# One-core decoder layer: reordered updates, scans and bias products, and other buffers for two weight halves

## What is computed

```python
def reference(x, mem, ...):
    h = rms_norm(x, norm_pre_mix)
    y = mixing_block(h, ...)            # four groups of 256 columns, see below
    x = x + rms_norm(y, norm_post_mix)
    h = rms_norm(x, norm_pre_xa)
    y = cross_attention(h, rms_norm(mem, norm_mem), xa_wq, xa_wkv, xa_wo)   # 4 heads, 256 memory tokens
    x = x + rms_norm(y, norm_post_xa)
    h = rms_norm(x, norm_pre_ffn)
    gu = h @ ffn_w_in                   # 1024 -> 2 x 2816
    y = (silu(gu[..., :2816]) * gu[..., 2816:]) @ ffn_w_out
    return x + rms_norm(y, norm_post_ffn)

def mixing_block(h, ...):
    u_s5, p_ml, p_rw, p_mb = split_cols(h @ w_in, ...)
    y = [s5_mixer(u_s5), mlstm_mixer(p_ml), rwkv7_mixer(p_rw), moba_mixer(p_mb, rel_bias)]
    return rms_norm_per_group(concatenate(y)) @ w_out
```

## Time and profile before

| | |
|---|---|
| median of 3 executions | 520.66 us (520.61 to 520.70) |
| profiled execution | 520.58 us, span 518.8 us |
| PE busy | 487.5 us (94%) |
| DVE busy | 378.5 us (73%) |
| ACT busy | 261.8 us (50%) |
| POOL busy | 167.0 us (32%) |
| moved by DMA | 79.33 MB, 153 GB/s |

### The profile page before, as it was taken

How to read it: one execution, slowest core, us unless ns; L and a number is a source line. 1 busy time by engine, 2 the same in 40 slices (tenths; PEclk the granted TensorE clock), 3 DMA queues, 4 the chain that set the end, 5 groups by cost and what they waited for, 6 DMA issues and landing times.

```text
span 518.8 us, 8480 instructions
## 1 busy us (share of the span) xinstructions
PE 487.5 (94%) x3494; PEld 446.7 (86%) x3494; DVE 378.5 (73%) x445; ACT 261.8 (50%) x412; POOL 167.0 (32%) x101
## 2 busy tenths in 40 slices
PE   0799999979999999999999999999999999999985
PEld 0789889978899878878999988999999999988874
DVE  5676797997756889587756466699999999962114
ACT  3598864412622334666856557544445444443333
POOL 0040227297669360000000000244334433443540
PEclk9999999989999999999999999999999999999999
DMA  8937328022031222626373460275445555545502
GB/s 334 375 96 233 150 81 322 3 82 81 1 100 64 82 82 81 244 82 220 120 270 125 155 223 26 82 265 183 163 167 195 205 173 200 199 162 198 208 1 81
DMA packets 12358, 79.33 MB, mean 153 GB/s; under 512 B 1440, under 2 KB 2080, under 8 KB 3488
## 3 DMA queue, kind: packets, MB, share of 16 engines
q1 hardware_dynamic: 12320, 78.79, 42.5%
HBM read 76.95 MB, written 1.84 MB: 152 GB/s over the span
## 4 chain that ended last, share of the span: by engine, by line
PE 84%; DVE 8%; ACT 3%; issue 2%; DMA 1%; POOLq 0%; POOL 0%; SPq 0%; DVEq 0%; ACTq 0%
PE bank L381 82%; DMA ring<-weights 1%; DVE arena L1668 1%; ACT w_high L356 1%; DVE vx L1695 1%; DVE arena L1485 1%; POOLq L90 0%; POOL w_rest L362 0%; DVE arena L1660 0%; DVE we_rest L362 0%; DVE arena L1661 0%; DVE wk_rest L362 0%; DVE arena L1839 0%; DVE wm_rest L362 0%; PE bank L814 0%
## 5 line engine op out<-in xcount | busy, mean ns | idle before, releaser
L362 POOL TENSOR_TENSOR w_rest<-ring,w_high 128x1024 fp32r<-128x1024 f32 x21 | 50.8, 2418 | 202.6 <-ACT w_high L356 202.6
L356 ACT ACTIVATE w_high<-ring 128x1024 fp32r<-128x1024 f32 x66 | 69.4, 1058 | 72.7 <-PE bank L381 72.6
L381 PE MATMUL bank<-h_high,w_high 128*128 128x256 f32 x384 | 102.9, 283 | 0.0
L381 PE MATMUL bank<-h_rest,w_high 128*128 128x256 f32 x352 | 99.6, 283 | 0.0
L381 PE MATMUL bank<-h_high,w_rest 128*128 128x256 f32 x320 | 90.6, 283 | 0.0
L362 DVE TENSOR_TENSOR w_rest<-ring,w_high 128x1024 fp32r<-128x1024 f32 x39 | 49.8, 1282 | 37.4 <-ACT w_high L356 37.4
L381 PEld LDWEIGHTS bank<-h_high,w_high 128*128 128x128 f32 x384 | 71.7, 192 | 0.5 <-issue 0.4
L381 PEld LDWEIGHTS bank<-h_rest,w_high 128*128 128x128 f32 x352 | 67.6, 192 | 0.0
L381 PE MATMUL bank<-arena 128*128 128x128 f32 (+7 forms) x496 | 59.2, 300 | 6.5 <-DVE arena L1691 4.5
L381 PEld LDWEIGHTS bank<-arena 128*128 128x128 f32 (+3 forms) x496 | 52.8, 182 | 12.6 <-DVE arena L1691 5.1
L381 PEld LDWEIGHTS bank<-h_high,w_rest 128*128 128x128 f32 x320 | 61.4, 192 | 0.0
(11 more groups left out here) (323 smaller groups left out, 1230.6 us busy)
## 6 DMA issues: line engine op xcount, KB each, us to landing
ring<-weights SPq DMA_DIRECT2D x50, 1024.0 KB, 5.0
third_slot<-weights SPq DMA_DIRECT2D x15, 1024.0 KB, 5.1
cst<-consts SPq DMA_DIRECT2D x1, 1664.0 KB, 12.6
gain<-gains SPq DMA_DIRECT2D x3, 512.0 KB, 5.8
par<-params SPq DMA_DIRECT2D x1, 1168.0 KB, 14.9
kx<-x_t SPq DMA_DIRECT2D x1, 1024.0 KB, 4.9
vx<-mem_t SPq DMA_DIRECT2D x1, 1024.0 KB, 10.3
xres<-x_rows SPq DMA_DIRECT2D x1, 1024.0 KB, 10.4
```

The source lines that it names most:

```text
L356: nc.scalar.activation(split_half(i)[0], raw_half(i), ACT.Copy).then_inc(S["w_high"], 1)
L362: e.tensor_tensor(rest_, raw_half(i), high.bitcast(F32), ALU.subtract).then_inc(rest_done(i)[0], 1)
L381: return nc.tensor.matmul(out_, lhsT, rhs, start=start, stop=stop, skip_group_check=True)
```

## The change

- The constant `onehot` moves to the front of the second block and comes with a DMA of its own, 33 rows, between weight slots 0 and 1 (`onehot_in`). The bias products `rel0` to `rel3` run right behind `x_sumsq`, ahead of `rw_wag`. PE's waits for the other constants and parameters move to just before `rw_w`.
- POOL makes the level-3 mask before `rotate_back(0)`.
- DVE: one rest, `level_update(1)`, one rest and then `scan(0)`; mLSTM's masks ahead of `scan(1)`; `solution(1)` ahead of S5's sigmoid and product.
- The group sum of S5 stands behind tile 1 of `wout`, not behind tile 0.
- The last two halves of `ffn_w_out` get the buffers `w_kx` and `w_wo[0]` for their high and rest parts, and ACT's split of them waits for no earlier product.

```diff
 CONST, NCONST = columns([
-    ("ones", P), ..., ("half_pi", 1), ("ident", P), ...
+    ("ones", P), ..., ("half_pi", 1), ("onehot", 384), ("ident", P), ...
-    ("onehot", 384),
 ])
-CONST_FIRST = CONST["ident"][0]
+CONST_FIRST, CONST_MORE = CONST["onehot"]
...
             if H_WO + HALF_BUFS <= i < H_FIN:
                 return w_wo[i - H_WO - HALF_BUFS]
+            if i >= NHALF - 2:
+                return (w_kx, w_wo[0])[i - NHALF + 2]
             return w_mid[i % MID_BUFS] if i < H_LATE else w_late[(i - H_LATE) % HALF_BUFS]
...
-            if before >= start:
+            if before >= start and i < NHALF - 2:
                 user = half_user[before]
...
             mm(o[:, 0:T], const("ones"), sq_x[:, 0, :]).then_inc(full[0], 1)
-            split_channel_major(0, "rw_wag", 1, h_split, lambda j: pe.wait_ge(S["h_rest"], j + 1))
-            split_channel_major(1, "rw_k", 0, h_split)
-            pe.wait_ge(S["consts_in"], 16)
-            pe.wait_ge(S["params_in"], 16)
+            pe.wait_ge(S["onehot_in"], 16)
             for h in range(NH):
                 o = pe_open(pe, f"rel{h}", 4 + h)
                 mm(o[:, 0:384], prm("rel", 33)[:, h:h + 1].to_broadcast([33, P]), const("onehot", 33)).then_inc(full[4 + h], 1)
+            split_channel_major(0, "rw_wag", 1, h_split, lambda j: pe.wait_ge(S["h_rest"], j + 1))
+            split_channel_major(1, "rw_k", 0, h_split)
             split_channel_major(2, "rw_r", 1, h_split)
...
             o = v3(pe_open(pe, "rw_w", 2)[:, :], T)
+            pe.wait_ge(S["consts_in"], 16)
+            pe.wait_ge(S["params_in"], 16)
             pe.wait_ge(S["rw_low"], 1)
...
             def group_sums(kt):
-                if kt == 0:
+                if kt == 1:
                     group_sumsq("gn_s5", 0, 3)
...
             for n in range(NSLOTS):
+                if n == 1:
+                    sp.dma_start(cst[0:33, CONST_FIRST:CONST_MORE], consts_d[0:33, CONST_FIRST:CONST_MORE]).then_inc(S["onehot_in"], 16)
                 if n == 2:
-                    sp.dma_start(cst[:, CONST_FIRST:], consts_d[:, CONST_FIRST:]).then_inc(S["consts_in"], 16)
+                    sp.dma_start(cst[:, CONST_MORE:], consts_d[:, CONST_MORE:]).then_inc(S["consts_in"], 16)
...
             level_mask(2)
+            level_mask(3)
             rotate_back(0)
-            level_mask(3)
             rotate(1)
...
+            rests(H_MID + 3)
+            level_update(1)
+            rests(H_MID + 4)
             scan(0)
-            rests(H_MID + 4)
-            level_update(1)
...
             level_update(2)
             rests(H_MID + 6)
-            scan(1)
-
             moved(dve, "g_col")
             dve.wait_ge(S["ml_qk"], 1)
...
                 last.then_inc(free_of(f"m_row{m}"), 1)
+            scan(1)
+
             level_update(3)
...
             rests(H_WKV + 10)
+            solution(1)
+            rests(H_WKV + 11)
             dve.wait_ge(S["s5_exp"], 1)
             sigmoid_of_exp(z5b, "s5_sig", 0).then_inc(S["s5_sig"], 1)
             dve.wait_ge(S["s5_sig"], 2)
             v.tensor_tensor(z5, z5y, z5b, ALU.mult).then_inc(S["s5_z"], 1)
-            rests(H_WKV + 11)
-            solution(1)
             group_gain(1, "ml")
```

More of the change, by code:

```diff
@@ L45 @@
 CONST, NCONST = columns([
-    ("ones", P), ("eps6", 1), ("eps12", 1), ("eps_gn", 1), ("eps6_xd", 1), ("round", 1), ("half_pi", 1), ("ident", P), ("pair_ones", P), ("strict", P), ("incl", P), ("causal_add", 384),
+    ("ones", P), ("eps6", 1), ("eps12", 1), ("eps_gn", 1), ("eps6_xd", 1), ("round", 1), ("half_pi", 1), ("onehot", 384), ("ident", P), ("pair_ones", P), ("strict", P), ("incl", P), ("causal_add", 384),
     ("levels", LEVELS * P), ("level0_t", P), ("time", T), ("head_sel", NH * P), ("pair_sel", 2 * P),
-    ("onehot", 384),
 ])
-CONST_FIRST = CONST["ident"][0]
+CONST_FIRST, CONST_MORE = CONST["onehot"]
 PARAM, NPARAM = columns([
@@ L263, in trunk_kernel @@
             ml_row_step ml_den mb_inv s5_step2 rw_tail s5_sig x_inv f_sig s5_sq s5_root ml_sq
-            ml_root rw_sq rw_root mb_sq mb_root diag_ready
+            ml_root rw_sq rw_root mb_sq mb_root diag_ready onehot_in
             w_high w_rest_even w_rest_odd w_rest_mid w_used high_ready act_rest y_rest h_high h_rest x_summed
```

## The result

| | kernel before | changed kernel |
|---|---|---|
| median, us | 520.97 (520.61 to 521.93, 8 executions) | 516.67 (515.90 to 518.88, 8 executions) |
| ratio, 95% interval | | 0.9925 (0.991 to 0.994) |
| profiled execution, us | 520.58 (span 518.8) | 518.57 (span 516.8, granted clock 0.990) |

The change is worth 4.3 us, about half of the 8.5 forecast, and 516.67 lies above the range of 509.6 to 516.0. The eight executions of the changed kernel fall in two groups: five at 515.9 to 516.8 with a mean granted clock of 0.996, and three at 518.2 to 518.9 with 0.990. The profiled one is of the second group, so its trace shows what that group pays.

What follows compares the result with a forecast made beforehand. TensorE was taken as the bound, 84% of the chain that ended last, so gains come from its idle gaps. 1.35 + 3.3 + 2.05 + 1.8 = 8.5 us gave 512.2 us, range 509.6 to 516.0.

Steps and rivals of the forecast that it cites:

- A: Opening: bias products first on TensorE, their constants in a small early transfer; 1.35 us gained, bounds 0 to 1.7.
- rival R1: Opening gives nothing because the clock falls in the new idle stretch before rw_v; 513.5 us, chance 0.12.
- B: Middle: level_update(1) before scan(0), level_mask(3) before rotate_back(0), mLSTM masks before scan(1); 3.3 us gained, bounds 5.2 and 1.9.
- S: End of the moved scan(0) on DVE, old time axis: 109.2 us taken, 107.3 without contention, 110.6 at worst.
- POOL's queue: POOL from rotate_back(0) at 7.09 through rotate(1) at 9.5 to level_mask(4), ending 135.8, just in time for level_p(4, 1) at 135.95.
- rival R2: POOL becomes the bound before level 4; B worth 1.5 to -0.6, time 515.1 us (514.0 to 516.1), chance 0.18.
- VectorE's order behind S: DVE's work after the scans: 8.55 + 1.8 us to the level-2 update at 119.5, level_p(3, 1) ending at 120.5.
- The clock: Sign for B: no 3.96 us idle, and TensorE's granted clock 1.00 throughout 100 to 115 us.
- C and D: C: solution(1) before S5's sigmoid, gn_s5 later, 2.05 us. D: last two weight halves in other buffers, 1.8 us.
- R3: No contention between DVE's scans and POOL: S = 107.3, time 510.3 us, chance 0.13.
- R4: Slower: POOL's operations double to 2.41 us, level_mask(4) ends at 151.5; time 527.7 us, chance 0.03.
- R5: Moves find the next wait where the old was; only C and D remain, in part: 519.7 to 517 us, chance 0.04.

Runs made afterwards that it cites:

- Bank 5: The changed kernel with s5_u's product in PSUM bank 5 instead of bank 1: 516.77 us, ratio 0.992; measured again 517.29 us, ratio 0.9929.
- The run over 128 rows: The changed kernel with bias products contracted over 128 rows, added rows zero, and all of onehot in the early transfer: 518.47 us, one execution.
- part B with the mask order: The kernel before with part B alone and level_mask(4) ahead of rotate_back(1) on POOL: 519.99 us, ratio 0.9998.
- both edits: The changed kernel with s5_u in bank 5 and level_mask(4) ahead of rotate_back(1): 513.75 us, ratio 0.9858; again 513.94 us, ratio 0.9868.
- Dummy products: 24 unread products around s5_out(0), added to the changed kernel: 515.93 us; added to the kernel before with part B alone: 520.14 us.

## Why the prediction was wrong, by its own steps

**A, forecast 1.35, measured 0.4 in the trace and 0.06 alone.** The step that failed is "then `s5_u` waits for its own half". It also waits for its bank: bank 1 is free only when DVE has mixed `rw_r`, and that was not in the sum. The mix stands behind the first rest in DVE's queue and ended at 45.20 before and 44.84 here, so `s5_u` could gain little more than 0.36. Bank 5 took 0.69 of this wait away. A second step, that hung on an "if", did not come: the clock was not raised by the bias products. They kept TensorE busy for 5.49 us, but the next 21 products kept the slow pace, and `rw_r` ended at 36.4 instead of 34.6. This cost next to nothing. The run over 128 rows shows the condition met, and with it the fall of the clock that rival R1 spoke of, behind an idle stretch of 2.33; yet the mix came at 43.90 and the end of `s5_u` moved by 0.07. That ACT is the chain there held in the changed kernel's trace only by a little: in five later traces with the new opening ACT first waited 0.16 to 0.46 for TensorE's `rw_wag`. The gain at the end of `s5_u` with bank 1 was 0 to 0.66 by the trace.

**B, forecast 3.3, measured about 1.0 with the clock up and nothing on average.** The wait and the cause of its going were right, and S was 108.7, 109.1 on the old axis, against 109.2. Behind it four terms failed.
- *POOL's queue*, "six operations, 9.5 taken": `rotate(1)` took 11.0 (115.07 to 126.08). The duration was borrowed from `rotate_back`, although `rotate(1)` has records of its own in the trace of before, and they add to 11.7. `rotate_back(0)` took 6.03 of the 7.09 put in, so the queue was only 0.7 late here (126.5 on the old axis for 125.8). One record of `rotate(1)` before is this:

```profile
114.06 3.93 POOL L1007 TENSOR_TENSOR arena<-arena 128x512 f32<-128x512 f32 x1
```

- `level_mask(4)`, 2.14 in the earlier trace rows, takes 4.11 when it falls beside DVE's `h_rest` (133.18, above); the forecast moved the mask and kept its price. This is the larger miss. "POOL is just in time" therefore became rival R2 where the clock stays up, with B inside its 1.5 to -0.6: the mask ends 0.10 before the product that waits for it. Reversing the order on POOL gave 1.0 more to part B alone, which shows that POOL was the bound there.
- *VectorE's order behind S*, "8.55 + 1.8": it took 8.86 to the first update (108.71 to 117.57) and four updates of 0.6, not three, so level 3 ended 0.8 later than forecast (121.34 for 120.5 in the trace of part B with the mask order; that trace was 0.3 ahead at 98 us, so 1.1 on the old axis). With that order part B gives 2.2 by the spans (518.8, 516.6) where the clock stays up, 1.9 without that lead, and the 1.1 accounts for most of the rest.
- *The clock*, "1.00 throughout 100 to 115". That held, but the forecast asked nothing about 115 to 131. It named a wait of 2 to 4 us before `level_p(3, .)` as a sign that it was right, and did not ask what the clock would do behind it. In the traced execution of the changed kernel the clock then stood at 0.50 for some ten microseconds: the products took 0.5 more on level 3 than at the upper level (2.88, 2.35 in the kernel with both edits), 1.8 more for `m_row` (3.76, 1.97) and 2.3 for `mb_v` (8.1, 5.9). That is 4.6. The wait for POOL that it covers gives 1.4 back (bank 5's trace needs 4.31 from its `qk` products at 134.34 to the product behind `level_p(4, .)`, the changed kernel's 2.91 from 139.28) and leaves 3.2; the two groups with bank 5 stand 3.0 apart. The kernel before pays for its 3.96 us as well, but more briefly (0.50 at 108, 1.00 again by 111):

```profile
111.00:112.00 1.00, 1.00 (x10) 1.00 (x10) 0.96 (x2) 0.38 (x1) 1.00 (x2) 1.00 0.00 0
```

So part B exchanged a sure short fall for a longer, uncertain one.

Dummy products took the group at 0.989 away in two kernels (4 and 11 executions), though a fall of some 3 us stayed in both traces. That the long fall follows on the idle and the short products is supported by this; that their absence is needed is not. The two edits together kept the clock up in 8 of 8 executions with that stretch unfilled, bank 5 alone in 5 of 12, the mask order with part B alone in 6 of 12. Up to 120 us, bank 5 alone and both edits issue the same instructions on TensorE, and their traces have level 3 start at 117.89 and 117.91, so no row shown here explains the difference, and I had no trace of bank 5's upper group to see where its fall is. This stays open. A possible reason why one kernel shows both outcomes is a rule of the Trainium skill, TensorE: Matmul & The Clock Gate, Part 1, by which the hardware's view of TensorE's activity runs freely and does not start with the kernel. The two groups agree with it; no run here shows it.

**C and D** came as forecast: 2.17 of 2.05 and 1.84 of 1.8 in the trace, and both together, 0.9921 alone, are the whole result (0.9925) within the intervals. R3 fell (the scans did slow), R4 fell (single POOL operations reached 3.7, but not the whole queue). R5 came nearest in its pattern: A and B found their next waits, and only C and D remained, but whole and not in part, so the time is just under its 517. It had a chance of 0.04, and the ten microseconds of low clock were in none of the rivals.

## What to carry to other kernels

A wait of the bound engine that is removed returns at the next one's queue: price every instruction of that queue from its own records, and price it again beside the neighbour it will have after the move, not the one it had. List for every product that is to start earlier all that it waits for, its output bank among them. Where a stretch of idle and thin products appears on TensorE, ask for the clock behind it, and judge such a change by many executions, for one trace shows one outcome.

## What the runs showed of the hardware that was not expected

- The same eight products over more rows left another clock behind: after 5.49 us of 33-row products the next were 0.21 apart, in every trace with them; after 4.82 us of 128-row products in the same place they were 0.12 apart (one trace).
- The fall need not begin in the idle stretch. Here it began near 120.6 us (the 0.64 of 120 to 122, worked out between 1.00 and 0.50), 1.7 after TensorE was busy again at 118.89; with part B alone it was at 0.97 over 118 to 120 and at 0.50 behind, so it began just before 120 there.
- Two scans of 0.66 took 1.58 and 1.51 beside POOL's mask, itself 3.27 for two where 2.15 is the other price; the next two took 0.66. The Trainium skill, SBUF — State Buffer, "Who interferes with whom", has these exclude each other, and the trace agrees.
